# Recurrence inputs fetched ahead, and narrow levels packed, in a decoder trunk on one core

## The chip, the core and the metric

The kernel runs on one core of a Trainium2 chip. A core has a matrix engine (TensorE, PE in the views; its weight loads are listed apart as PEld), VectorE (DVE), ScalarE (ACT), GpSimd (POOL) and SyncE (SP), which here issues DMAs. The metric is the device time of one launch in microseconds, as the median of several runs. Lower is better.

## What is computed

One layer of a hybrid decoder for a prompt of 2048 tokens and eight samples of eight tokens. A normed input is projected by one wide matrix; half of the heads do sparse attention, the other half a gated linear recurrence; then come the output projection and an MLP. What matters here is the recurrence of the prompt, four heads with a 128x128 state each:

```python
f = lb + (1.0 - lb) * jax.nn.sigmoid(f_logit)
logf = jnp.log(f)
k = 1.0 - f
def step(S, inp):
    qc, kc, vc, gc = inp
    b = jnp.cumsum(gc, axis=2)
    inter = jnp.einsum('bhtd,bhdv->bhtv', qc * jnp.exp(b), S)
    diff = b[:, :, :, None, :] - b[:, :, None, :, :]
    decay = jnp.exp(jnp.where(mask[:, :, None], diff, -jnp.inf))
    A = jnp.einsum('bhtd,bhtsd,bhsd->bhts', qc, decay, kc)
    o = inter + jnp.einsum('bhts,bhsv->bhtv', A, vc)
    bl = b[:, :, -1:, :]
    S = jnp.exp(bl[:, :, 0])[..., None] * S + jnp.einsum('bhsd,bhsv->bhdv', kc * jnp.exp(bl - b), vc)
    return S, o
```

The kernel uses chunks of 128 tokens, 16 of them.

## The kernel before

The stages follow one another: `projections`, then `attention`, whose first part is `recurrence_prompt`, and later `output_and_mlp`. Between stages, and at the end of `recurrence_prompt`, all engines meet.

**Projections.** Four tiles `i` of 512 tokens, each with 28 steps `p`. A step multiplies two of the eight row blocks of one of seven column groups (`kv`, `rg`, `rf`, `q`, `rq`, `qi`, `ri`, four steps each) by all 512 tokens, 24 matmuls. Every step needs its 128x1024 piece of weights in two parts: the high part (`hi`, L332) by ScalarE, the low part (`lo`, L480) by VectorE from the high one, both two steps ahead. `hi(g)` waits until TensorE is done with step g-2. Steps 12 to 19 also carry the forget gate of one head after another: in even steps VectorE turns exp(-z) into f (`forget`, L511, L512, L544); in odd steps ScalarE makes k and log f (L443, L445) ahead of its `hi`, and VectorE runs the scan that gives b (`decay`, L549) behind its `lo`. k goes to the scratch `rkT` and b to `rbT`, by SP. In steps 19 to 26 of tiles 0 to 2 TensorE turns the next tile's rows (L671), and VectorE makes their low part (`turned_low`, L501, tile `hT`). In tile 2 VectorE also does so for the sample's rows in step 19 (L653), and in tile 3 each step has eight or four further matmuls for the sample.

**The prompt's recurrence.** A chunk's pair weights A are built by levels. A level l splits the tokens into groups of 2m = 2 << l; its factors are exp(ref - (b - log k)) for the earlier half of a group and q * exp(b - ref) for the later half, with ref the b between the halves. One matmul per head gives all products of a level, and VectorE picks those that belong to it into `pair_weights` (`copy_predicated`, L1115 and L1121). The order of levels is 6, 5, 0, 1, 2, 3, 4. The two widest are put by small matmuls over the k·q product into one bank (L1170, L1177), and picked together (the joined pick); the other five are matmuls of 128x128 by 128 (L1185), with a bank and a pick each. There are four banks for six slots.

Per chunk GpSimd subtracts (12 instructions, L961 and L962), ScalarE takes exponentials (L1008, L1009, L1015), and VectorE multiplies the later halves by q (L1132). ScalarE also takes log k (L991) and VectorE subtracts it from b (L1100), for the next chunk; GpSimd waits for that. Then come q·exp b (L1127), the decayed keys and their transposes (L997, L1193, L1031), the outputs (L1203, L1204), the new state (L1208, L1061), the norm (L975 to L1079) and the gate (`mix`, L1087). Each engine's order is the order of the code, chunk by chunk; chunks 0, 1, 14 and 15 are written out and the others are a loop of two.

SP loads k, b, q, v and the gate's rows two chunks ahead, one queue, in the order of `next_inputs`; between the loads for chunks 2 and 3, and again between those for 3 and 4, stand the sample's small loads (`index_inputs`, L897 to L906). The first loads of the stage are issued at its start. Ahead of the chunks GpSimd has two memsets and four indirect gathers, and VectorE makes the gathers' indices (L1046 to L1052).

## Time and profile before

| | us |
|---|---|
| median of 3 runs | 4038.43 |
| lowest and highest | 4038.22, 4041.91 |
| the profiled execution's own time | 4044.13 |
| its span | 4042.4 |
| projections, in the span | 0 to 680.8 |
| prompt's recurrence, in the span | 680.8 to 914 |

| engine | busy us | share of the span |
|---|---|---|
| TensorE | 3576.2 | 88% |
| VectorE | 2794.6 | 69% |
| ScalarE | 2219.3 | 55% |
| GpSimd | 1048.2 | 26% |

The busy shares are averages over stages. In a timeline row the first number is the start in us from the span's start, the second the length from the first to the last of a merged group; brackets hold the idle time ahead of the group and what ended it. In a row of waits the numbers are the sum of the waits in us, how many, and the longest. In a row by stretch each engine has busy time and the number of instructions; PEclk is the granted clock of TensorE, where 1.00 is its upper level of 2.4 GHz and 0.50 the lower of 1.2 GHz.

### The profile page before, as it was taken

The numbers are of one execution on the slowest core, as the hardware profiler recorded it, in microseconds if no ns is written. First come the engines' busy times: TensorE is split into PE (matmuls) and PEld (weight loads), VectorE is DVE, ScalarE is ACT, GpSimd is POOL, SyncE is SP. The second block draws the span as 40 slices with busy tenths as digits, with TensorE's granted clock in tenths as the row PEclk, the third lists the DMA queues.
The fourth block names the chain that finished last, engine by engine and source line by source line (L and its number), as shares of the span: only waits on it lengthen the run. The fifth ranks groups of instructions, "written<-read, shape, count | busy, mean of one in ns | idle before, by whom it ended". The sixth has DMA issues, their size and how long they took to land. (4 is left out here: it accounts for less than half of the span.)

```text
span 4042.4 us, 52687 instructions
## 1 busy us (share of the span) xinstructions
PE 3576.2 (88%) x18026; PEld 2856.8 (71%) x18027; DVE 2794.6 (69%) x4745; ACT 2219.3 (55%) x3701; POOL 1048.2 (26%) x1120
## 2 busy tenths in 40 slices
PE   8999998889777489875599998989999998999998
PEld 7878786777655235454488886868888887888886
DVE  6675655887888789888678885665556544555565
ACT  3333323776678589887567774335455444443232
POOL 0000001664311011100256730215556551000011
PEclk9999998999877799986699999989999999999999
DMA  6555444435200244424456633567667656554464
GB/s 170 166 150 156 132 125 149 118 102 157 64 23 21 73 148 173 157 99 122 121 197 216 222 132 131 198 215 222 191 218 233 201 179 197 183 186 147 137 217 138
DMA packets 387885, 624.83 MB, mean 155 GB/s; under 512 B 97560, under 2 KB 216440, under 8 KB 379320
## 3 DMA queue, kind: packets, MB, share of 16 engines
q1 hardware_dynamic: 309848, 312.05, 26.0%
q0 software_dynamic: 77376, 309.63, 22.9%
q8 instruction: 137, 2.24, 0.2%
q14 instruction: 108, 0.88, 0.1%
q10 hardware_dynamic: 416, 0.02, 0.0%
HBM read 444.81 MB, written 176.77 MB: 154 GB/s over the span
## 5 line engine op out<-in xcount | busy, mean ns | idle before, releaser
L3814 PE MATMUL up_acc<-x_parts_first,w_up_parts 128*128 128x512 f32 x1536 | 361.4, 395 | 14.1 <-DVE w_up_parts L3564 14.1
L738 PE MATMUL accumulated<-hT,w_in_parts 128*128 128x512 f32 x1536 | 361.3, 395 | 2.1 <-DVE w_in_parts L480 2.1
L3814 PEld LDWEIGHTS up_acc<-x_parts_first,w_up_parts 128*128 128x128 f32 x1536 | 293.3, 191 | 76.6 <-DVE w_up_parts L3564 15.3
L738 PEld LDWEIGHTS accumulated<-hT,w_in_parts 128*128 128x128 f32 x1536 | 290.6, 190 | 65.3 <-DVE w_in_parts L480 3.8
L2800 DVE TENSOR_SCALAR_CACHE_REDUCE junk_dve<-score,candidate 128x2048 bf16<-128x2048 f32 (+6 forms) x224 | 328.5, 1505 | 8.5 <-DVE candidate L2786 8.0
L3905 PE MATMUL down_acc<-w_down_parts_even,hidden_parts 128*128 128x512 f32 x1344 | 314.6, 391 | 14.0 <-DVE hidden_parts L3600 11.8
L3905 PE MATMUL down_acc<-w_down_parts_odd,hidden_parts 128*128 128x512 f32 x1344 | 312.7, 390 | 0.0
L3905 PEld LDWEIGHTS down_acc<-w_down_parts_even,hidden_parts 128*128 128x128 f32 x1344 | 252.9, 189 | 68.3 <-issue 15.9
L2723 ACT ACTIVATE junk_act<-score,candidate 128x1920 bf16<-128x1920 f32 (+6 forms) x224 | 286.4, 1294 | 19.6 <-DVEq L2787 15.6
L3366 ACT ACTIVATE hidden_parts<-hidden_raw 128x1024 fp32r<-128x1024 f32 x112 | 118.6, 1059 | 312.3 <-PE down_acc L3905 289.8
L3905 PEld LDWEIGHTS down_acc<-w_down_parts_odd,hidden_parts 128*128 128x128 f32 x1344 | 251.8, 188 | 53.2 <-issue 1.0
L332 ACT ACTIVATE w_in_parts<-w_in_raw 128x1024 fp32r<-128x1024 f32 (+1 forms) x112 | 113.6, 1014 | 296.5 <-PE accumulated L734 121.2
L480 DVE TENSOR_TENSOR w_in_parts<-w_in_raw,w_in_parts 128x1024 fp32r<-128x1024 f32 (+1 forms) x112 | 130.8, 1169 | 203.4 <-ACT w_in_parts L332 202.1
L3564 DVE TENSOR_TENSOR w_up_parts<-up_raw,w_up_parts 128x512 fp32r<-128x512 f32 x224 | 176.0, 786 | 113.0 <-ACT w_up_parts L3344 111.5
L734 PE MATMUL accumulated<-w_in_parts,hT 128*128 128x512 f32 (+1 forms) x1152 | 239.5, 366 | 1.7 <-DVE hT L501 1.7
L2108 DVE TENSOR_TENSOR probs_T<-p_T,probs_T 128x512 fp32r<-128x512 f32 x272 | 183.8, 688 | 73.7 <-ACT probs_T L2032 72.3
L734 PEld LDWEIGHTS accumulated<-w_in_parts,hT 128*128 128x128 f32 x1152 | 200.2, 188 | 32.3 <-issue 3.2
L3600 DVE TENSOR_TENSOR hidden_parts<-hidden_raw,hidden_parts 128x1024 fp32r<-128x1024 f32 x112 | 138.1, 1233 | 111.9 <-ACT hidden_parts L3366 111.6
L2032 ACT ACTIVATE probs_T<-p_T 128x512 fp32r<-128x512 f32 x272 | 156.9, 594 | 94.1 <-PE p_T L1968 93.1
L1390 PE MATMUL dots<-ki_high,qi_parts 128*128 128x512 f32 (+3 forms) x304 | 146.8, 485 | 68.9 <-ACT relu L1412 67.1
L3263 POOL DMA_DIRECT2D hidden_raw<-scratch_hs x112 | 60.1, 537 | 536.4 <-DVE hidden_parts L3600 536.4
L1459 DVE SCALAR_TENSOR_TENSOR score<-relu,wi,score 128x1024 f32<-128x1024 f32 (+7 forms) x154 | 180.4, 1171 | 24.5 <-ACT relu L1412 7.7
(541 smaller groups left out, 8685.2 us busy)
## 6 DMA issues: line engine op xcount, KB each, us to landing
hidden_raw<-scratch_hs POOLq DMA_DIRECT2D x112, 512.0 KB, 4.6
w_in_raw<-in_w_in SPq DMA_DIRECT2D x80, 512.0 KB, 4.1
up_raw<-scratch_ws SPq DMA_DIRECT2D x128, 256.0 KB, 2.9
scratch_hs<-hidden_even POOLq DMA_DIRECT2D x112, 256.0 KB, 5.0
scratch_hs<-hidden_odd POOLq DMA_DIRECT2D x112, 256.0 KB, 4.9
up_raw<-in_w_up SPq DMA_DIRECT2D x96, 256.0 KB, 5.6
weight_sums<-in_w_down POOLq DMA_DIRECT2D x16, 1024.0 KB, 5.3
scratch_wt<-weight_sums POOLq DMA_DIRECT2D x16, 1024.0 KB, 5.7
```

The source lines that it names most:

```text
L734: mm = pe.matmul(z, h[:, a, k, n * P:(n + 1) * P], w2[:, g % 2, b, k2 * w:(k2 + 1) * w], start=(first and j == 0), stop=(last and j == 2))
L738: mm = pe.matmul(z, w2[:, g % 2, b, k2 * ST + n * P:k2 * ST + (n + 1) * P], h[:, a, k, :], start=(first and j == 0), stop=(last and j == 2))
L1390: pe.matmul(dots[:, u % DB, c:c + w], qs[:, b, h, :], kh[:, k], start=True, stop=False)
L1459: dve.scalar_tensor_tensor(s, r, wi[:, i, h:h + 1], s, ALU.mult, ALU.add).then_inc(acc_done, 1)
L2032: act.activation(ET[:, s % 3, 0, :], pT[:, turn_at[s] % 3, :], ACT.Copy).then_inc(th_rdy, 1)
L2108: dve.tensor_tensor(ET[:, s % 3, 1, :], pT[:, turn_at[s] % 3, :], ET[:, s % 3, 0, :].bitcast(F32), ALU.subtract).then_inc(tl_rdy, 1)
L2723: act.activation(ja[:, n % 2, 0:WIDTH[i]], score[:, SOFF[i]:SOFF[i + 1]], ACT.Sign, bias=cf[:, c:c + 1], accum_out=cnt[:, c:c + 1]).then_i ...
L2800: dve.tensor_scalar(jd[:, n % 2, 0:WIDTH[i]], score[:, SOFF[i]:SOFF[i + 1]], cf[:, c:c + 1], None, ALU.is_ge, ALU.add, accum_out=cnt[:, c: ...
L3564: dve.tensor_tensor(out, raw[:, g % RAW, :], high.bitcast(F32), ALU.subtract).then_inc(lo_rdy, 1)
L3600: dve.tensor_tensor(ap[:, s % A_PARTS, 1, :], araw[:, s % A_RAW, :], ap[:, s % A_PARTS, 0, :].bitcast(F32), ALU.subtract).then_inc(a_lo, 1)
L3814: mm = pe.matmul(up_bank(n), wp[:, n % SLOTS, b, q * P:(q + 1) * P], X(i)[:, a, q, :], start=(q == 0 and (a, b) == (0, 0)), stop=(q == QUA ...
L3905: mm = pe.matmul(down_bank(s), ap[:, s % A_PARTS, a, j * P:(j + 1) * P], B(ph)[:, j, b, :], start=(j == 0 and (a, b) == (0, 0)), stop=(j = ...
```

## The change

1. **b less log k.** Projections now compute it: ScalarE takes `Ln` of `k_stage` into the tile `exp_neg_g`, VectorE subtracts it from the scan's b in place, and SP stores it to a new scratch `rbkT`. The recurrence loads it with b; its own `log_k` and `less_log_k` are gone, and GpSimd waits for the load only.
2. **Three wide levels in one bank.** The order is 6, 5, 4, 0, 1, 2, 3. Levels 4, 5 and 6 share the bank and the pick of the k·q product; TensorE waits for the third multiply, and then does level 4 first, in 16 matmuls of 16 by 16. Slots go from six to five.
3. **Packed later halves.** For levels 0 to 3 the multiply by q writes the later halves into the new tile `later_factors`. The level's matmul streams these 64 columns a head, and the pick reads 256 packed columns.
4. **Fetched inputs.** The recurrence's inputs for chunks 0 and 1, its masks and the identity are loaded by GpSimd's queue in tile 3 of the projections, in 15 DMAs, into memory that tile 2's `hT` has left. SP's own first loads are gone. GpSimd's memsets move behind chunk 0 and its gathers behind chunk 1; the index arithmetic on VectorE moves behind chunk 0.

The diff, cut to its core:

```diff
 # projections: SP, GpSimd, ScalarE, VectorE
+                    if p in (14, 16, 18, 20):
+                        c = (p - 14) // 2
+                        sp.wait_ge(bk_rdy, 4 * i + c + 1)
+                        out(sc["rbkT"][c, :, tok], exg[:, c, :], bk_out[c])
...
+                pool.wait_ge(w_used, PER * END)
...
+                for par in range(2):
+                    own = slice(par * P, (par + 1) * P)
+                    for dst, src in (("r_k", "rkT"), ("r_b", "rbT"), ("b_less_log_k", "rbkT"), ("r_q", "rqT")):
+                        pool.dma_start(head[dst][:, par, :, :], sc[src][:, :, own].rearrange("h p t -> p h t")).then_inc(head_in, 16)
...
                             act.activation(fw[:, 1, :], fw[:, 0, :], ACT.Ln).then_inc(ln_done, 1)
+                            act.wait_ge(k_rdy, 4 * i + c + 1)
+                            act.wait_ge(g_rdy, 4 * i + c + 1)
+                            act.activation(exg[:, c, :], kst[:, c % 2, :], ACT.Ln, bias=least[:, 0:1]).then_inc(lnk_done, 1)
                         hi(PER * i + p + 2)
...
                     dve.tensor_tensor_scan(bst[:, c % 2, :], smask[:, :], fw[:, 1, :], 0.0, ALU.mult, ALU.add).then_inc(b_rdy, 1)
+                    dve.wait_ge(lnk_done, 4 * i + c + 1)
+                    dve.wait_ge(b_rdy, 4 * i + c + 1)
+                    dve.tensor_tensor(exg[:, c, :], bst[:, c % 2, :], exg[:, c, :], ALU.subtract).then_inc(bk_rdy, 1)
 # recurrence
-    ORDER = [6, 5, 0, 1, 2, 3, 4]
-    SLOTS = LEVELS - 1
+    ORDER = [6, 5, 4, 0, 1, 2, 3]
+    JOINED = 3
+    SLOTS = 1 + LEVELS - JOINED
...
+                    turned(bk, "rbkT", g, par, b_in)
                     turned(bt, "rbT", g, par, b_in)
...
-                    pool.wait_ge(b_in[par], 16 * j + 16)
-                    pool.wait_ge(bk_rdy, g + 1)
+                    pool.wait_ge(b_in[par], 32 * j + 32)
...
-                            if not is_last(g):
-                                log_k(g + 1, j + par, 1 - par)
...
-                        dve.tensor_tensor(x, x, qs, ALU.mult).then_inc(x_rdy, 1)
-                        if n >= 2:
-                            pick(n - 2)
+                        if n < JOINED:
+                            dve.tensor_tensor(x, x, qs, ALU.mult).then_inc(x_rdy, 1)
+                        else:
...
+                            dve.tensor_tensor(later[:, n - JOINED, :, :].rearrange("p h t -> p (h t)").rearrange("p (n m) -> p n m", m=1 << ORDER[n]),
+                                              x, qs, ALU.mult).then_inc(x_rdy, 1)
+                        if n >= JOINED:
+                            pick(n - JOINED)
...
                             middle(g + 1, j + par, 1 - par)
-                            less_log_k(g + 1, 1 - par)
...
-                    for n in range(2):
+                    pe.wait_ge(x_rdy, LEVELS * g + JOINED)
+                    for n in reversed(range(JOINED)):
                         m = 1 << ORDER[n]
-                        pe.wait_ge(x_rdy, LEVELS * g + n + 1)
...
-                            x = X[:, ORDER[slot + 1], h * P:(h + 1) * P]
-                            mm = pe.matmul(o[:, h * P:(h + 1) * P], x, x, start=True, stop=True)
+                            x = X[:, ORDER[slot + JOINED - 1], h * P:(h + 1) * P]
+                            mm = pe.matmul(o[:, h * P // 2:(h + 1) * P // 2], x, later[:, slot - 1, h, :], start=True, stop=True)
```

On VectorE, in an odd step of tile 1 of the projections, before:

```order
L544 TENSOR_SCALAR forget<-exp_neg,lb_work 128x512
L480 TENSOR_TENSOR w_in_parts<-w_in_raw,w_in_parts 128x1024
L549 SCALAR_TENSOR_TENSOR b_stage<-scan_mask,forget 128x512
L485 TENSOR_SCALAR row_stats<-row_stats 128x4
L480 TENSOR_TENSOR w_in_parts<-w_in_raw,w_in_parts 128x1024
```

and after:

```order
L571 TENSOR_SCALAR forget<-exp_neg,lb_work 128x512
L507 TENSOR_TENSOR w_in_parts<-w_in_raw,w_in_parts 128x1024
L576 SCALAR_TENSOR_TENSOR b_stage<-scan_mask,forget 128x512
L579 TENSOR_TENSOR exp_neg_g<-b_stage,exp_neg_g 128x512
L512 TENSOR_SCALAR row_stats<-row_stats 128x4
L507 TENSOR_TENSOR w_in_parts<-w_in_raw,w_in_parts 128x1024
```

The subtract (`exp_neg_g<-b_stage,exp_neg_g`) stands between the scan and the low part of the following step's weights.

On TensorE, the levels of chunk 1 of the recurrence, before:

```order
L1170 MATMUL levels<-r_q,r_k 128x128 x4
L1177 MATMUL levels<-level_factors 64x64 x4
L1177 MATMUL levels<-level_factors 32x32 x8
L1185 MATMUL levels<-level_factors 128x128 x12
L1193 MATMUL kd_T<-identR,k_decayed 128x128 x4
L1185 MATMUL levels<-level_factors 128x128 x8
```

and after:

```order
L1187 MATMUL levels<-r_q,r_k 128x128 x4
L1194 MATMUL levels<-level_factors 16x16 x16
L1194 MATMUL levels<-level_factors 32x32 x8
L1194 MATMUL levels<-level_factors 64x64 x4
L1202 MATMUL levels<-later_factors,level_factors 128x64 x12
L1208 MATMUL kd_T<-identR,k_decayed 128x128 x4
L1202 MATMUL levels<-later_factors,level_factors 128x64 x4
```

Sixteen products of 16 by 16 come in ahead, four of 128 columns go, and the rest of these stream 64 columns; behind the transposes stands one level where two stood. The program's matmuls count once here, and twice in the trace, where each is two instructions.

## Rows read from the trace of the kernel before

**Rows 1.** Waits from 20 to 680 us: sum, times, longest (us)

```profile
PE accumulated L671 <- DVE hT L501: 10.1, 6, 1.9
PE accumulated L671 <- DVE hT_sample L653: 3.9, 1, 3.9
```

**Rows 2.** Timeline of VectorE in tile 1 of the projections

```profile
252.60 1.23 DVE L480 TENSOR_TENSOR w_in_parts<-w_in_raw,w_in_parts 128x1024 fp32r<-128x1024 f32 x1 [2.26 <-ACT w_in_parts L332]
...
266.27 1.23 DVE L480 TENSOR_TENSOR w_in_parts<-w_in_raw,w_in_parts 128x1024 fp32r<-128x1024 f32 x1 [1.02 <-ACT w_in_parts L332]
...
295.64 0.74 DVE L501 SCALAR_TENSOR_TENSOR hT<-accumulated,gain_pre_mix,hT 128x512 fp32r<-128x512 f32 x1
```

**Rows 3.** Timeline of TensorE in tiles 1 and 2

```profile
288.83 5.73 PE L738 MATMUL accumulated<-hT,w_in_parts 128*128 128x512 f32 x24 [1.07 <-DVE w_in_parts L480]
296.44 0.66 PE L671 MATMUL accumulated<-identA,x_sb 128*128 128x128 f32 x4 [1.87 <-DVE hT L501]
296.86 7.34 PE L738 MATMUL accumulated<-hT,w_in_parts 128*128 128x512 f32 x24
...
450.22 7.73 PE L738 MATMUL accumulated<-hT,w_in_parts 128*128 128x512 f32 x24
```

**Rows 4.** Busy time by stretch: us, then each engine, clock, DMA share, GB/s

```profile
296.80:304.20 7.40, 7.40 (x29) 5.89 (x28) 5.76 (x5) 0.69 (x1) 0.00 (x0) 0.77 0.40 106
...
786.00:812.00 26.00, 21.36 (x204) 19.44 (x202) 22.54 (x55) 20.57 (x65) 18.61 (x24) 1.00 0.40 121
```

**Rows 5.** Timeline of one chunk in the loop

```profile
804.63 2.63 DVE L1132 TENSOR_TENSOR level_factors<-level_factors,r_q 128x256 f32<-128x256 f32 x3
...
805.88 1.06 PE L1177 MATMUL levels<-level_factors 128*64 128x64 f32 x24
...
807.19 0.72 DVE L1115 COPY_PREDICATED pair_weights<-level_mask_joined,levels 128x512 f32<-128x512 int32 x1
...
807.81 0.41 DVE L1132 TENSOR_TENSOR level_factors<-level_factors,r_q 128x256 f32<-128x256 f32 x1
...
814.81 0.42 DVE L1121 COPY_PREDICATED pair_weights<-level_masks_second,levels 128x256 f32<-128x256 int32 x1
...
815.28 0.49 PE L1203 MATMUL o<-state,q_exp_b 128*128 128x128 f32 x2 [0.99 <-DVE pair_weights L1121]
```

**Rows 6.** Groups by form, 786 to 812.35 us: busy us, mean ns, idle before

```profile
L991 ACT ACTIVATE log_k<-r_k,least_k 128x512 f32<-128x512 f32 x2 | 1.4, 710 | 0.0
L1100 DVE TENSOR_TENSOR b_less_log_k<-r_b,log_k 128x512 f32<-128x512 f32 x2 | 1.4, 684 | 0.0
```

**Rows 7.** Timeline of chunk 0 of the recurrence

```profile
686.49 0.69 DVE L1100 TENSOR_TENSOR b_less_log_k<-r_b,log_k 128x512 f32<-128x512 f32 x1
...
687.22 0.35 ACT L1008 ACTIVATE level_factors<-b_less_log_k,r_b 128x64 f32<-128x64 f32 x1 [1.65 <-DVE b_less_log_k L1100]
...
691.49 0.64 POOL L961 TENSOR_TENSOR less_ref<-r_b,b_less_log_k 128x256 f32<-128x256 f32 x1
...
699.74 0.63 ACT L1015 ACTIVATE level_factors<-less_ref 128x512 f32<-128x512 f32 x1 [0.57 <-POOL less_ref L962]
...
706.84 0.46 PE L1203 MATMUL o<-state,q_exp_b 128*128 128x128 f32 x2 [0.77 <-DVE pair_weights L1121]
```

**Rows 8.** Timeline of TensorE: first outputs of chunks 1, 2, 3 and 15

```profile
719.65 0.46 PE L1203 MATMUL o<-state,q_exp_b 128*128 128x128 f32 x2 [1.04 <-DVE pair_weights L1121]
...
736.53 0.49 PE L1203 MATMUL o<-state,q_exp_b 128*128 128x128 f32 x2 [0.75 <-DVE pair_weights L1121]
...
750.20 0.49 PE L1203 MATMUL o<-state,q_exp_b 128*128 128x128 f32 x2 [1.00 <-DVE pair_weights L1121]
...
904.77 0.46 PE L1203 MATMUL o<-state,q_exp_b 128*128 128x128 f32 x2 [0.75 <-DVE pair_weights L1121]
```

**Rows 9.** Timeline of ScalarE in chunk 2

```profile
726.52 0.72 ACT L991 ACTIVATE log_k<-r_k,least_k 128x512 f32<-128x512 f32 x1 [4.68 <-DMA r_k<-scratch_rkT]
```

**Rows 10.** Timeline of TensorE: groups of small matmuls

```profile
660.79 1.00 PE L704 MATMUL accumulated<-foldA,x_sb 128*128 128x64 f32 x8
...
693.89 0.64 PE L1177 MATMUL levels<-level_factors 128*32 128x32 f32 x16 [3.02 <-DVE level_factors L1132]
```

More of the change, by code:

```diff
@@ L84, in own_semaphores, with projections @@
         stage(nc, *args)
-def projections(nc, io, sc):
+def projections(nc, io, sc, head):
     RAW = 3
@@ L795, in recurrence_prompt @@
         sb, ps, sem = memory(nc, ctx)
-        qt, kt, bt = (sb(n, [P, 2, RH, P]) for n in ("r_q", "r_k", "r_b"))
-        vt, gt = sb("r_v", [P, 2, RH, P]), sb("r_g", [P, 2, RH, P])
-        ident = sb("identR", [P, P])
-        joined = sb("level_mask_joined", [P, 1, P], I32)
-        second = sb("level_masks_second", [P, SLOTS - 1, RH * P // 2], I32)
-        lk, least = sb("log_k", [P, RH, P]), sb("least_k", [P, 1])
-        bk = sb("b_less_log_k", [P, 2, RH, P])
+        qt, kt, bt, bk, vt, gt = (head[n] for n in ("r_q", "r_k", "r_b", "b_less_log_k", "r_v", "r_g"))
+        ident, joined, second = (head[n] for n in ("identR", "level_mask_joined", "level_masks_second"))
+        sb("head_inputs", [P, (HEAD_SKIP + HEAD_BYTES - BEFORE_HEAD) // 4])
         mid = sb("minus_b_mid", [P, 2, RH])
@@ L830, in recurrence_prompt, with chunks @@
         qb, wd, kn = (ahead[n] for n in ("qi_blocks", "wi_rows", "ki_new"))
-        def chunks(eng, body):
+        def chunks(eng, body, between=None):
             for par in range(2):
                 body(par, 0, par)
+                if between:
+                    between(par)
             with eng.Fori(1, NCH // 2 - 1) as j:
@@ L1148, in _, with index_rows @@
                 middle(0, 0, 0)
-                less_log_k(0, 0)
-                chunks(dve, body)
+                def index_rows(par):
+                    if par == 1:
+                        return
+                    pages, odd, base = (ahead[n] for n in ("pages", "odd_half", "base"))
+                    dve.wait_ge(x_pages, 32)
+                    dve.tensor_scalar(base[:, 0, :], pages[:, :], 16.0, odd[:, 0:1], ALU.mult, ALU.add).then_inc(x_base, 1)
+                    dve.tensor_scalar(base[:, 1, :], pages[:, :], 8.0, odd[:, 1:2], ALU.mult, ALU.add).then_inc(x_base, 1)
+                    dve.wait_ge(x_base, 2)
+                    for c in range(8):
+                        dve.tensor_scalar(gidx[:, :, c], base[:, 0, :], float(c), None, ALU.add).then_inc(x_idx, 1)
+                    for c in range(4):
+                        dve.tensor_scalar(gkv[:, :, c], base[:, 1, :], float(c), None, ALU.add).then_inc(x_idx, 1)
+                chunks(dve, body, index_rows)
                 add_state(NCH - 1, 1)
@@ L1241, with attention @@
 PROBS_SKIP = 136000
-def attention(nc, io, sc):
+HEAD_SKIP, BEFORE_HEAD = 49152, 8800
+HEAD_TILES = (*((n, [P, 2, RH, P], F32) for n in ("r_q", "r_k", "r_b", "b_less_log_k", "r_v", "r_g")), ("identR", [P, P], F32),
+              ("level_mask_joined", [P, 1, P], I32), ("level_masks_second", [P, LEVELS - 3, RH * P // 2], I32))
+HEAD_BYTES = 4 * sum(math.prod(shape[1:]) for _, shape, _ in HEAD_TILES)
+def attention(nc, io, sc, head):
     with ExitStack() as ctx:
@@ L1269, in attention @@
                      "ident": at("identP", [P, P])[:, :], "fold": at("foldP", [P, DH])[:, :]}
-        own_semaphores(nc, recurrence_prompt, io, sc, gidx, gkv, ahead)
+        own_semaphores(nc, recurrence_prompt, io, sc, gidx, gkv, ahead, head)
         with ExitStack() as pctx:
@@ L3975, in constants @@
             "bucket_of": (np.arange(BUCKETS)[:, None] == bucket[None, :]).astype(np.float32),
[L3976 removed]
+            "levels": lev.astype(np.int32), "levels_joined": (lev[:, 0:1] | lev[:, 5:6] | lev[:, 6:7] | lev[:, 7:8]).astype(np.int32), "levels_second": second, "later": (s > t).astype(np.int32)}
 def views(io):
@@ L3991, in trunk @@
     io = views(io)
-    own_semaphores(nc, projections, io, sc)
-    attention(nc, io, sc)
+    with ExitStack() as place:
+        at = memory(nc, place)[0]
+        at("head_skip", [P, HEAD_SKIP // 4])
+        head = {n: at(n, shape, dt) for n, shape, dt in HEAD_TILES}
+    own_semaphores(nc, projections, io, sc, head)
+    attention(nc, io, sc, head)
     own_semaphores(nc, output_and_mlp, io, sc)
```

120 lines of the change are left out of this document (54 added, 66 removed).

## The prediction

> **What bounds the kernel now.** I read the page's busy slices first (TensorE is near full except in two places), then the stretches, then the waits of the two stages that the diff touches, then their timelines. The change edits only the projections (0 to 680.8 us of the span) and the prompt's recurrence (680.8 to 914), which run one after the other with a barrier between and after them. So a microsecond lost or won in either moves the end of the span by about as much, and the sum is made per stage.
>
> The projections look bound by TensorE, but where TensorE stands still, VectorE is late: it waits for `hT` and for the sample's `hT` [rows 1]. In tile 1 VectorE is on a chain without a gap: weights' low parts (`lo`), `forget`, a round trip through ScalarE (k, Ln, then the high part of the next weights) that VectorE waits 2.26 us for, `lo`, scan [rows 2]. It has one piece of slack in the phase, 1.02 us at 266.27, and its last link, the subtract of hT that ends at 296.38, releases TensorE [rows 2, 3]. The stall also costs clock: the 24 products behind it take 7.34 us, where 5.7 is usual (the group at 288.83 takes that), because the granted clock falls to 0.77 over that stretch; after the 3.94 us stall of tile 2 it is 7.73 us [rows 3, 4].
>
> In the recurrence no engine is full: of 26.0 us (two chunks) VectorE is busy 22.5, TensorE 21.4, ScalarE 20.6, GpSimd 18.6 [rows 4]. One chunk takes 12.9 us, by a ring: the last pick of a chunk releases TensorE's outputs, new state, k·q and wide levels (about 4.7 us), while VectorE does mix, q·exp b and three multiplies; then picks and multiplies alternate with TensorE's levels up to the next last pick [rows 5].
>
> **Added to the projections.** Each of 4 tiles by 4 heads gets one more Ln of 128x512 on ScalarE, between the Ln of forget and the weights' high part, and one more subtract of 128x512 on VectorE behind the scan. Same shapes now take 710 and 684 ns [rows 6]; successive instructions overlap by some 0.09, so 0.62 and 0.61 on the engine. The subtract needs the scan to have ended, and loses that overlap and a semaphore's time: 0.13. Both lie on the chain above, since VectorE waits for ScalarE's high part: 1.36 us a head, 5.4 a tile. Tiles 0 and 1 have the 1.0 us of slack once: +4.4 each. Tile 2 has sample work in that place, and TensorE waits at its end for the sample's hT, which VectorE reaches late [rows 1]; only 0.25 is absorbed: +5.2. A longer stall should leave more of the following step at the low clock, as 7.73 against 7.34 shows: +0.4 in tiles 0 and 1. In tile 3 TensorE's steps are longer for the sample's products, and the chain has gaps of 2 to 3.5 us: +0.2. Sum **+15.0**. Below: 12, if ScalarE's Ln hides in the wait for k and the clock costs nothing. Above: 17, if tile 3 or the clock takes more. The 16 stores of `rbkT` stand on SP's queue behind loads that already wait for a later `lo`, so nothing waits for them. The 15 fetches on GpSimd's queue run in tile 3, where that engine is idle, and move 3 MB beside weights loaded two steps ahead: 0.
>
> **Taken from the recurrence's start.** Today the first loads are issued at 680.8; b less log k starts at 686.49, the wide factors at 687.22, and GpSimd, behind four indirect gathers, starts at 691.49; the last exponential of chunk 0 starts at 699.74 and its outputs at 706.84 [rows 7]. With inputs there at 680.8, ScalarE has its table and exp b by 682.7, the wide factors by 684.7; GpSimd starts at once, its first two pairs are ready in time, and the rest follow the exponentials by 1.4 us a pair, to a last exponential at about 691.3. Then multiplies, three narrow levels, transposes and the last level: outputs at about 695.5 at full clock. TensorE is cold here, so I take 696.3: **-10.5** (-8 to -12). VectorE's 14 small index instructions move behind chunk 0; TensorE's outputs, state and k·q of chunk 0 cover most of their 1.5 us. The gathers move behind chunk 1 and make GpSimd 1.3 us late for chunk 2, and in chunk 1 the loop's shorter form gains it back: **-0.3** for chunk 1.
>
> **Chunks 2 and 3.** Outputs start at 706.84, 719.65, 736.53, 750.20: chunk 2 takes 16.9 us, chunk 3 takes 13.7 [rows 7, 8]. ScalarE waits 4.68 us for r_k, whose load stands behind 20 sample loads on SP [rows 9]. log k and this wait go. Next late is b and b less log k of chunks 3 and 4, queued behind the same sample loads; with the whole stage 11 us earlier they land about when `minus_b_mid` wants them. With GpSimd's 1.3 us and about 1 us for chunk 3's b: **-3.7** (-1 to -4.7).
>
> **The loop, 12 more chunks.** Take the end of the third multiply as 0. Today the joined pick starts within 0.47 us of it and the last pick ends at +8.0 [rows 5]. Changed: VectorE loses the subtract (0.61) and one pick (0.34), ScalarE the Ln (0.62). But TensorE now starts the wide levels only after the third multiply, and has 32 more narrow matmul instructions. The present 24 (8 of 64 columns, 16 of 32) take 1.06 [rows 5], of which the last instruction's own length is 0.2; split by columns that is 0.053 and 0.027 apart, and even at the low clock 16 of 32 columns take 0.64, at most 0.03 apart [rows 10]. So 16 columns cost 0.013 each if the spacing falls further, 0.027 if not: 0.4 to 0.9, I take 0.65. So the joined pick starts at +1.95, and state, multiplies and picks follow; pick 2 waits for TensorE (1.4 after its multiply), the last pick starts at +7.85 and ends at +8.3. Halving the moving columns gains nearly nothing: 8 instructions that load 128 columns and stream 64 take 1.00 us [rows 10], the same as eight of 128. What shortens the ring is the other part: GpSimd no longer waits for VectorE's b less log k and works while VectorE picks, so q·exp b and the first multiply run uncontended; the three multiplies take 2.6 us beside GpSimd now [rows 5], but 0.41 us each alone. Third multiply at +12.1 to +12.5, and TensorE's k·q ends at +12.0, so there is no more than that to win. 12.3 against 12.88 (904.77 less 750.20, by 12) is **-7.0**; between 12.0 and 12.9, so -10.6 to 0.
>
> On the narrow products, the trace has no 16-column form, and its spacing falls with the columns down to 32 [rows 5, 10]. The Trainium skill, TensorE: Matmul & The Clock Gate, Back-to-back issue gap, states a floor of about 25 ns for 1 to 64 columns; by it the 32 would cost 0.8 us and the loop's gain would be 5 us; no run here shows it yet.
>
> **Sum.** 15.0 - 10.5 - 0.3 - 3.7 - 7.0 = -6.5 us. The profiled execution took 4044.1 (span 4042.4), so 4037.6 by its own time; the median of the runs is 4038.4, so **4031.9**.
>
> **Rivals.**
> - *The loop stays at 12.9.* Contention moves from the first multiplies to the later ones, since GpSimd's two early pairs fall beside them, and the ring is as long as before. For: the last pick ends at +8.3 against +8.0, later than today. Against: GpSimd idles 7.4 us in 26 [rows 4]. Gives 15.0 - 14.5 = +0.5: 4039. Chance 0.22.
> The Trainium skill, Advanced Engine Details and Errata, VectorE Performance Modes, says that VectorE's second SBUF port is shared with GpSimd and the two block each other; the 2.6 us for three multiplies agree, and by the rule work that moves beside other multiplies gives the loss back there, which is this rival.
> - *More gained, or less lost.* The loop reaches 12.0 (TensorE's bound), or VectorE's added work costs 12 and not 15. For: I place most waits at their worst. Gives -13, up to -18 with both: 4025, down to 4020. Chance 0.28.
> - *Narrow products dominate.* The 32 instructions of 16 columns sit in the ring, before the joined pick, with nothing beside them. If each costs as much as one of 128 columns, 0.107, they take 3.4 us for my 0.65, times 14 chunks, +38: 4070. It turns the sum slower by 8 us from 0.053 each. Against: the 32-column ones go at 0.027. A milder way to the same side is a late b for several chunks. Chance 0.10.
> - *Forecast*: chance 0.40.
>
> **Numbers.** 4031.9. A measurement of this kernel tells about 0.2% (8.1 us) from no change, so the threshold is 4030.3, close to my sum: a third of the forecast's own chance lies beyond it. Faster 0.28 + 0.13 = 0.41; same 0.27 + 0.22 = 0.49; slower 0.10. Range: 4022 (both gains larger, all but the far end) to 4044 (loop unchanged, projections 17, start -8).
>
> **What would show it.** The projections' end at about 696 for 680.8; TensorE's stall before the turned rows longer by 2 us or more in tiles 0 to 2, with `w_in_parts` at odd steps waiting 2.9 us for 2.26. The first outputs 15 to 16 us after the barrier, for 26. No wait for r_k in chunks 2 and 3. In the loop, 12.3 us from output to output; the joined pick waiting over 1 us; narrow products (56 instructions) in 1.5 to 2.0 us. Wrong would be: no shift of the projections' end (ScalarE and VectorE had cover that I missed), or a loop over 13 us.

## The result, and the profile after

The changed kernel took 4077.9 us (median of four runs, 4072.7 to 4085.5) against 4039.6 us for the kernel before, run beside it: a ratio of 1.0094, with a 95% interval of 1.0081 to 1.0106. The forecast was 4031.9 us; its range ended at 4044, and slower had a chance of 0.10. The profiled execution of the changed kernel took 4073.4 us, 4.5 less than its median, and that of the kernel before 4044.1, 4.5 more than its median. The spans, 4071.5 us against 4042.4, so differ by 29 us and not by the medians' 38, and the traces explain these 29.

| us from the span's start | before | changed | e1 | e3 | e7 |
|---|---|---|---|---|---|
| VectorE's first instruction of the recurrence | 680.85 | 692.88 | 692.34 | 692.36 | 677.21 |
| first outputs, chunk 0 | 706.84 | 710.05 | 707.55 | 707.19 | 693.09 |
| first outputs, chunk 3 | 750.20 | 754.12 | 749.46 | 750.47 | 735.55 |
| first outputs, chunk 15 | 904.77 | 931.94 | 904.48 | 904.75 | 890.18 |
| TensorE's first instruction of the next stage | 917.49 | 947.15 | 917.16 | 917.43 | 902.89 |
| span | 4042.4 | 4071.5 | 4041.7 | 4042.9 | 4028.8 |

e1, e3 and e7 are experiments that follow. First the loop of twelve chunks by stretch, in the kernel before:

```profile
750.20:904.77 154.57, 127.40 (x1200) 116.05 (x1201) 133.37 (x323) 119.99 (x375) 108.83 (x140) 1.00 0.38 112
```

and in the changed kernel:

```profile
754.12:931.94 177.82, 149.51 (x1488) 141.89 (x1489) 127.29 (x300) 114.91 (x367) 109.68 (x140) 0.77 0.37 112
```

What follows the recurrence is the same to 0.6 us (3124.9 and 3124.4 us, by the table). The loop grew by 23.3 us, 14.82 us a chunk for 12.88, and the third number from the end of its row points at why: TensorE's granted clock was 1.00, and is 0.77. One chunk of the changed kernel, TensorE's timeline; L1202 are the packed products:

```profile
785.61 0.63 PE L1218 MATMUL o<-state,q_exp_b 128*128 128x128 f32 x2
...
788.84 1.30 PE L1194 MATMUL levels<-level_factors 128*16 128x16 f32 x56
790.07 1.10 PE L1202 MATMUL levels<-later_factors,level_factors 128*128 128x64 f32 x8
792.44 2.14 PE L1202 MATMUL levels<-later_factors,level_factors 128*128 128x64 f32 x16 [1.27 <-DVE later_factors L1137]
...
795.23 1.81 PE L1202 MATMUL levels<-later_factors,level_factors 128*128 128x64 f32 x8
```

and the clock over it, by stretch:

```profile
788.00:792.00 4.00, 3.17 (x73) 2.81 (x71) 2.74 (x8) 2.25 (x5) 4.00 (x6) 1.00 0.51 149
792.00:798.00 6.00, 4.89 (x29) 4.70 (x30) 3.78 (x14) 3.15 (x12) 1.87 (x3) 0.69 0.40 119
798.00:801.50 3.50, 3.50 (x19) 3.50 (x19) 3.17 (x7) 2.90 (x10) 2.42 (x3) 0.55 0.40 128
801.50:805.50 4.00, 3.93 (x79) 3.56 (x78) 2.65 (x5) 3.05 (x11) 4.00 (x6) 1.00 0.47 149
```

The clock is at the upper level (2.4 GHz) when outputs, state and k·q have just run; it falls to the lower one (1.2 GHz) during the packed products, and comes back only in the next chunk's outputs and state. So the same eight packed products take 1.10 us and 1.81 us within one chunk, and two outputs 0.63 us for the 0.39 of a chunk that starts at the upper level (at 769.01). At full clock the 56 narrow products take 1.30 us for the 1.06 us of 24 [rows 5]: the rival that I feared is not there, 32 more cost 0.24 us.

The projections end 12.0 us later. TensorE's waits in them (sum, times, longest), in the kernel before one that [rows 1] leaves out:

```profile
PE accumulated L738 <- DVE w_in_parts L480: 2.1, 2, 1.1
```

and in the changed kernel the three largest:

```profile
PE accumulated L769 <- DVE w_in_parts L507: 9.8, 14, 2.2
PE accumulated L702 <- DVE hT L528: 8.9, 10, 1.7
PE accumulated L702 <- DVE hT_sample L684: 6.1, 1, 6.1
```

VectorE's timeline in tile 1 of the changed kernel:

```profile
256.61 1.23 DVE L507 TENSOR_TENSOR w_in_parts<-w_in_raw,w_in_parts 128x1024 fp32r<-128x1024 f32 x1 [2.87 <-ACT w_in_parts L357]
...
259.07 0.69 DVE L579 TENSOR_TENSOR exp_neg_g<-b_stage,exp_neg_g 128x512 f32<-128x512 f32 x1
...
268.15 1.23 DVE L507 TENSOR_TENSOR w_in_parts<-w_in_raw,w_in_parts 128x1024 fp32r<-128x1024 f32 x1 [2.87 <-ACT w_in_parts L357]
```

As the prediction had it, the round trip through ScalarE takes 2.87 us for 2.26 [rows 2], and the new subtract stands behind the scan; a head takes 11.54 us. The lateness shows at w_in_parts (9.8 us for 2.1); at hT, where the prediction looked for it in tiles 0 and 1, TensorE waits no longer than before (8.9 us for 10.1).

### The profile page after: what moved, and what is told of

The parts are those of the page before. It is cut to its first block and busy times, and to the rows that moved or that the text cites. A ratio compares the mean times of both kernels' runs of the same rounds, so it can differ in the third digit from the quotient of the medians.

```text
span 4071.5 us, 53472 instructions
## 1 busy us (share of the span) xinstructions
PE 3604.1 (89%) x18410; PEld 2886.5 (71%) x18411; DVE 2794.0 (69%) x4729; ACT 2220.3 (55%) x3701; POOL 1058.9 (26%) x1135
## 3 DMA queue, kind: packets, MB, share of 16 engines
q8 instruction: 138, 2.26, 0.2%
```

## The experiments

Medians are of 4 to 11 runs each, ratios to the kernel before run in the same comparison (medians 4041.7, 4040.9 and 4041.4 us for e1 to e4, e5 to e8, e9 to e12), with 95% intervals. The theory after the first look: the halved products cost nothing in time and take the clock away.

**e1, full width.** In the changed kernel:

```diff
-mm = pe.matmul(o[:, h * P // 2:(h + 1) * P // 2], x, later[:, slot - 1, h, :], start=True, stop=True)
+twice = later[:, slot - 1, h:h + 1, :].to_broadcast([P, 2, P // 2])
+mm = pe.matmul(o[:, h * P // 2:h * P // 2 + P].rearrange("p (n m) -> p n m", n=2), x, twice, start=True, stop=True, skip_group_check=True)
```

> The changed kernel with one edit: each product of a single level (L1202) streams 128 columns again, its 64 packed ones twice, so that TensorE streams as many columns there as in the kernel before; its output, VectorE's work and every wait are as in the changed kernel. Theory A (TensorE's granted clock falls in the loop because the halved products give it less to stream): the clock of the loop goes from 0.79 back to about 0.97, the chunk from 14.8 to about 13.4 us, the total from 4078 to about 4060. Rival B (it falls because TensorE stands idle before the later joined pick, whatever it streams): clock and total stay, 4073 to 4083. Rival C (the low clock is the chip's own state and not the kernel's doing): clock varies from run to run without regard to the edit.

Measured: 4045.6 us, ratio 1.0013 [1.0004, 1.0022], so 32 us less than the changed kernel, and lower than theory A had given. By stretch:

```profile
749.46:904.48 155.02, 118.39 (x1488) 108.23 (x1489) 126.64 (x300) 115.12 (x370) 108.86 (x140) 1.00 0.43 129
```

TensorE's waits from 749.4 to 904.5 us:

```profile
PE levels L1203 <- DVE later_factors L1137: 18.1, 21, 1.5
PE levels L1194 <- DVE level_factors L1133: 10.4, 12, 1.5
PE o L1219 <- DVE pair_weights L1121: 8.8, 13, 0.8
```

One group of its products:

```profile
797.56 1.16 PE L1203 MATMUL levels<-later_factors,level_factors 128*128 128x128 f32 x8 [0.26 <-DVE later_factors L1137]
```

The clock is 1.00 and the chunk 12.92 us. TensorE waits longer here, 37.3 us over the loop, than in the changed kernel (18.1, 2.1 and 8.8 for the same three waits), and is busy for 76% of the time against 84%. These sums alone would not settle rival B, since the low clock itself lengthens what TensorE does and so shortens its waits. So take one chunk in each from the first outputs on, both at the upper level. The changed kernel, then what followed at once:

```profile
768.46:777.00 8.54, 6.78 (x102) 6.34 (x102) 7.19 (x19) 6.98 (x25) 6.45 (x9) 1.00 0.51 154
...
777.40:782.89 5.49, 4.61 (x22) 4.24 (x22) 2.84 (x8) 2.93 (x12) 2.23 (x4) 0.50 0.33 96
```

and e1, the same piece and then the whole chunk:

```profile
762.57:771.10 8.53, 6.81 (x101) 6.32 (x102) 7.18 (x19) 6.89 (x24) 6.51 (x9) 1.00 0.52 154
...
762.57:775.12 12.55, 9.91 (x124) 9.03 (x124) 10.47 (x26) 9.58 (x32) 9.16 (x12) 1.00 0.49 146
```

TensorE stands still for 1.76 us in the one piece and 1.72 in the other, and only in the changed kernel does the clock fall after it. Rival B falls. What the halving saved is 0.06 us in eight products (1.10 for 1.16).

**e2, the kernel before with half width.**

```diff
-mm = pe.matmul(o[:, h * P:(h + 1) * P], x, x, start=True, stop=True)
+_, xs, _ = halves(x, ORDER[slot + 1])
+_, os, _ = halves(o[:, h * P:(h + 1) * P], ORDER[slot + 1])
+mm = pe.matmul(os, x, xs, start=True, stop=True, skip_group_check=True)
```

> The kernel before with one edit: each product of a single level (L1185) streams only the 64 columns that the pick reads, read and written with a stride in their old places; nothing is packed, nothing else moves. Theory A: the loop's clock falls below 0.9 and its chunk grows from 12.9 to over 13.5 us: total 4038 + 8 to + 20. Rival B: TensorE waits no longer than before, so the clock stays at 0.99 and the total at 4036 to 4040.

Measured: 4089.4 us, ratio 1.0121 [1.0106, 1.0137]. More than expected: this edit alone, which takes work away, costs 48 us. Its loop by stretch:

```profile
755.95:943.28 187.33, 164.26 (x1200) 154.85 (x1201) 131.88 (x323) 118.85 (x372) 103.86 (x140) 0.76 0.31 93
```

and eight of its products at either level, in TensorE's timeline:

```profile
782.54 1.11 PE L1187 MATMUL levels<-level_factors 128*128 128x64 f32 x8 [0.83 <-DVE level_factors L1132]
...
829.40 1.81 PE L1187 MATMUL levels<-level_factors 128*128 128x64 f32 x8
```

**e5, other products in the gaps.** In the changed kernel, before slot 2 and before the outputs:

```diff
+for h in range(RH):
+    pe.matmul(o[:, h * P:(h + 1) * P], ident[:, :], vt[:, par, h, :], start=True, stop=True, skip_group_check=True)
```

> The changed kernel with packed products of 64 columns as they are, plus 8 products in each chunk that nobody reads (identity times r_v, 128 columns, 16 matmul instructions), put where TensorE waits: four before its wait for the second single level, four before its wait for the last pick. They add as many columns as the packing took away. Theory A (the clock follows how much TensorE streams, in whatever form): the loop's granted clock returns to 0.97 or more, the chunk to 13.0 to 13.6 us (the fillers may delay the outputs by up to 0.5), total 4046 to 4056. Rival D (it is the 64-column form itself, its instructions too short for their 128-column weight loads): clock stays near 0.8, and the fillers run at the low clock too and lengthen the chunk: 4078 or more.

Measured: 4052.1 us, ratio 1.0026 [1.0015, 1.0038]; 26 us less than the changed kernel for 16 instructions more a chunk, on whose results nothing rests. The loop by stretch:

```profile
754.52:907.40 152.88, 135.41 (x1682) 128.07 (x1681) 123.68 (x301) 114.99 (x369) 109.15 (x140) 1.00 0.44 132
```

Clock 1.00, and 12.74 us a chunk. Rival D falls: the 64-column form itself does no harm. By itself e5 would also fit rival B, since the fillers take up waits; it is e1 that excludes B. With three kernels changed in opposite directions and the clock following each time, rival C falls too: the mean clock of the whole span is 0.919 to 0.927 in all eight runs of the changed kernel and e2, and 0.933 or more in every run of every other kernel. Chunk 0 pays for the fillers: 19.6 us from the barrier to the outputs at a clock of 0.50, for 15.2 at 0.63 in e1. So from the barrier to the next stage e5 takes 227.3 us for e1's 224.8, although its loop is shorter; the medians are 6.5 us apart, and the rest of that is open.

**e3, two wide levels and nothing packed.** The multiply in place, the waits of the narrow products and the strided pick are also as in the kernel before; b less log k from the projections and the fetch remain.

```diff
-ORDER = [6, 5, 4, 0, 1, 2, 3]
-JOINED = 3
+ORDER = [6, 5, 0, 1, 2, 3, 4]
+JOINED = 2
...
-mm = pe.matmul(o[:, h * P // 2:(h + 1) * P // 2], x, later[:, slot - 1, h, :], start=True, stop=True)
+mm = pe.matmul(o[:, h * P:(h + 1) * P], x, x, start=True, stop=True)
```

> The changed kernel without the three joined levels and without the packed halves: b less log k from the projections and the fetched inputs remain, the levels are multiplied, put through TensorE and picked as in the kernel before. Projections 12 us longer, first outputs 8 to 9 us sooner after the barrier than in the kernel before, chunks 2 and 3 some 4 us shorter, the loop 12.9 us a chunk or a little less, without subtract and Ln (12.5): sum -0.5 to -6. Total 4033 to 4040. Were the loop's loss due to b less log k coming from memory rather than to the narrow products, the total would stay above 4060.

Measured: 4045.2 us, ratio 1.0012 [1.0003, 1.0021], 5 to 12 us above what was expected. Outputs come 14.8 us after the barrier for 26.0 (-11.2). But chunks 2 and 3 take 30.76 us for 30.55, and the loop 12.86 us a chunk: the subtract and the Ln are gone from it, and it is no shorter. Its time equals e1's, so the third wide level and the packing, with full columns, are together worth nothing that shows. GpSimd's timeline ahead of chunk 2:

```profile
715.34 1.02 POOL L987 DMA_INDIRECT ki_rows<-in_cache_idx_k,gather_idx  x1 [0.16 <-issue]
...
719.19 0.94 POOL L987 DMA_INDIRECT ki_rows<-in_cache_idx_k,gather_idx  x1 [0.30 <-issue]
```

and VectorE's in chunk 2:

```profile
722.67 5.36 DVE L1131 TENSOR_TENSOR level_factors<-level_factors,r_q 128x256 f32<-128x256 f32 x3
```

**e8, the gathers behind the last chunk.** e3 with this in GpSimd's program:

```diff
-                    else:
-                        pool.wait_ge(x_idx, 12)
-                        for n in range(4):
-                            pool.indirect_dma_start(ahead["ki_rows"][:, n, :], None, io["cache_idx_k"][0].rearrange("a (c r) d -> (a c) (r d)", c=16),
...
                 chunks(pool, body, index_rows)
+                pool.wait_ge(x_idx, 12)
+                for n in range(4):
+                    pool.indirect_dma_start(ahead["ki_rows"][:, n, :], None, io["cache_idx_k"][0].rearrange("a (c r) d -> (a c) (r d)", c=16),
...
```

> e3_two_wide_unpacked with the four gathers of index rows put behind the last chunk. In e3 chunk 2 took 18.2 us while GpSimd, 4.8 us late behind the gathers, subtracted beside VectorE's multiplies (5.36 us for three). If the gathers cause that: chunk 2 in 13 to 14 us, total 4 to 5 us below e3, 4041. If chunk 2 is long for a late r_b or r_k: no change.

Measured: 4042.2 us, ratio 1.0003 [0.9994, 1.0012], 3 us below e3. The same three multiplies take 2.57 us:

```profile
724.86 2.57 DVE L1130 TENSOR_TENSOR level_factors<-level_factors,r_q 128x256 f32<-128x256 f32 x3
```

and outputs 1 to 3 are 27.44 us apart (722.62 to 750.06) for 30.76. So the four gathers, 4.8 us on GpSimd, had eaten what chunks 2 and 3 would have won.

**e6 and e9, less on GpSimd.** Both are e3 with less work for GpSimd from chunk 1 on (chunk 0 keeps both lines); the factors are then made from old differences. e6 leaves out the second subtraction of each level, e9 replaces both by one of four columns:

```diff
+if isinstance(g, int) and g == 0:
...
+else:
+    pool.tensor_tensor(of, ref, kf, ALU.subtract).then_inc(sub_done, 2)
```

```diff
+if isinstance(g, int) and g == 0:
...
+else:
+    pool.tensor_tensor(dif[:, n % 2, 0:4], bt[:, par, 0, 0:4], bt[:, par, 0, 0:4], ALU.subtract).then_inc(sub_done, 2)
```

> e3_two_wide_unpacked with GpSimd's second subtraction of each level (L978 there, 128x256) left out from chunk 1 on, so that the upper halves of the factors are made from older differences and the result is not the reference's; all waits remain. Theory (the loop stays at 12.86 us in e3 because GpSimd works beside VectorE and stretches its multiplies: q times exp b 1.04 to 1.10 us for 0.69, three multiplies 2.6 for 1.2): the multiplies shorten and the chunk falls to 12.0 to 12.4 us, total 5 to 10 us below e3. Rival (the loop is bound by the alternation of VectorE and TensorE and not by GpSimd): 12.8 us, total as e3, 4045.

> e3_two_wide_unpacked with GpSimd's two subtractions of each level replaced by one of four columns from chunk 1 on: its load is gone from the loop, all waits remain, the factors are made from old differences and the result is not the reference's. With half of that load gone (e6) the chunk fell from 12.86 to 12.61 us only, though the three multiplies were still 2.6 us. If contention with GpSimd is what keeps the loop long, the multiplies of all levels fall to 0.41 us and the chunk to 12.0 or less (total 4033 or less). If TensorE's outputs, state, k.q and joined levels (5.1 us from the last pick to the joined one) cover the early multiplies and only the later ones count, the chunk is 12.2 to 12.6 us and the total 4036 to 4041.

Measured: e6 4041.0 us, ratio 1.0000 [0.9991, 1.0009], 12.61 us a chunk; e9 4036.1 us, ratio 0.9987 [0.9978, 0.9996]. e9's outputs of chunks 4 to 13 are 12.14 us apart (874.59 less 765.29, by 9). Both chunks lie between what the two theories had given; e9's total is at the low end of the second theory's. VectorE's groups by form from 763.6 to 891.5 us, some ten chunks, in the kernel before:

```profile
L1132 DVE TENSOR_TENSOR level_factors<-level_factors,r_q 128x256 f32<-128x256 f32 x70 | 44.0, 651 | 0.0
...
L1127 DVE TENSOR_TENSOR q_exp_b<-r_q,exp_b 128x512 f32<-128x512 f32 x10 | 7.8, 777 | 4.9 <-DVE mix_rows L1087 4.9
```

in e3:

```profile
L1131 DVE TENSOR_TENSOR level_factors<-level_factors,r_q 128x256 f32<-128x256 f32 x70 | 48.4, 713 | 0.0
...
L1126 DVE TENSOR_TENSOR q_exp_b<-r_q,exp_b 128x512 f32<-128x512 f32 x10 | 10.5, 1046 | 5.3 <-DVE mix_rows L1093 5.3
```

and in e9:

```profile
L1134 DVE TENSOR_TENSOR level_factors<-level_factors,r_q 128x256 f32<-128x256 f32 x73 | 28.6, 416 | 0.0
...
L1129 DVE TENSOR_TENSOR q_exp_b<-r_q,exp_b 128x512 f32<-128x512 f32 x11 | 7.6, 692 | 5.5 <-DVE mix_rows L1096 5.5
...
L1117 DVE COPY_PREDICATED pair_weights<-level_mask_joined,levels 128x512 f32<-128x512 int32 x10 | 7.4, 739 | 18.0 <-PE levels L1190 18.0
```

Taking the subtract (6.9 us in ten chunks) off VectorE left its other multiplies longer by 7.1 us (4.4 and 2.7), which ate all of it. That they contend with GpSimd is shown by e9: with GpSimd's load gone a multiply takes 416 ns for 713. The Trainium skill, Advanced Engine Details and Errata, VectorE Performance Modes, says that GpSimd and VectorE's two-port instructions block each other at a shared port; the 416 ns for 713 agree with blocking, but which port these multiplies use no run here shows. The chunk only falls to 12.14 us, because VectorE then waits 1.8 us a chunk for TensorE's joined levels (the last row). So both causes hold, in turn: GpSimd for 0.7 us, and TensorE behind it.

**e4 and e7, the fetch alone.** e4 is e3 with the change's part of the projections taken back, and in the recurrence's loop, on ScalarE and on VectorE:

```diff
+log_k(g + 1, j + par, 1 - par)
...
+less_log_k(g + 1, 1 - par)
```

e7 is e4 with the gathers as in e8, and in `less_log_k`

```diff
 dve.wait_ge(lk_rdy, g + 1)
-dve.wait_ge(mid_rdy, g + 1)
+dve.sem_inc(spare, 1)
```

> The kernel before with only the inputs of the first two chunks and the constants fetched during the projections (and the index rows moved behind chunks 0 and 1); log k and the subtract stay in the recurrence. Projections as before (0), first outputs 6 to 9 us sooner after the barrier, chunk 2 perhaps still waiting for r_k: total 4028 to 4034, so 4 to 10 us faster than before. If the fetch on GpSimd's queue disturbs the projections' weights, it is 4038 or more.

> e4_fetched_only with the four gathers of index rows put on GpSimd's queue behind the last chunk, where it is idle, and without the extra wait for minus_b_mid that e4's subtract had. If the gathers (4.8 us on GpSimd in chunk 2) and that wait explain why e4 gained 3 us and not 10: chunk 2 in 13.5 us for 16.1 in before's and e4's pattern, loop 12.9 us for e4's 13.4, total 4026 to 4032. If the loop's 13.4 us in e4 has another cause, it stays at 13.4 and the total at 4034 to 4038.

Measured: e4 4038.6 us, ratio 0.9993 [0.9984, 1.0002], 5 us above the expected range; e7 4032.2 us, ratio 0.9981 [0.9972, 0.9991], just above its own. Outputs 15.9 us after the barrier in both. e4's loop takes 13.39 us a chunk and e7's 12.89; which of e7's two edits gave this was not separated, though e3 and e8, which differ by the gathers alone, have nearly the same loop (12.86 and 12.83). e7 beats both kernels.

**e10 and e11, the projections' part alone.** e10 is e7 with Ln, subtract and store of the change in the projections, read by nobody:

```diff
+act.wait_ge(k_rdy, 4 * i + c + 1)
+act.wait_ge(g_rdy, 4 * i + c + 1)
+act.activation(exg[:, c, :], kst[:, c % 2, :], ACT.Ln, bias=least[:, 0:1]).then_inc(lnk_done, 1)
...
+dve.wait_ge(lnk_done, 4 * i + c + 1)
+dve.wait_ge(b_rdy, 4 * i + c + 1)
+dve.tensor_tensor(exg[:, c, :], bst[:, c % 2, :], exg[:, c, :], ALU.subtract).then_inc(bk_rdy, 1)
```

and e11 is e10 without the last three of these lines; the store waits for `lnk_done` there.

> e7_fetched_late_rows plus the projections' part of the change alone: Ln of k, subtract and store of b less log k, which the recurrence does not read. It prices that part with the recurrence unchanged. By the prediction's chain (both on the way of VectorE's next weights): +15 us, between 12 and 17: total 4044 to 4049. By the profiled runs so far (barrier at 691.5 to 695.0 with it, 677.2 to 680.9 without): 12 to 15. If part of the loss was the transfer of the result or its fetch, less than 10.

> e10_both_places without VectorE's subtract: ScalarE's extra Ln and the store remain in the projections, the recurrence is as in e7. If the chain runs through ScalarE's high part to VectorE's low part, as the prediction has it, Ln costs 0.6 us of the 1.36 a head: about 6 us over e7, total 4037 to 4040. If Ln hides behind VectorE's own work and the subtract alone is late: 0 to 2 us over e7. If ScalarE is the bound: as e10.

Measured: e10 4049.0 us, ratio 1.0021 [1.0012, 1.0030]; e11 4038.3 us, ratio 0.9993 [0.9984, 1.0002]. So 16.8 and 6.1 us above e7. The recurrence's first VectorE instruction in e7's timeline:

```profile
677.21 0.06 DVE L1055 MEMSET least_k<- 128x1 f32 x1 [13.04 <-PEq L83]
```

in e11's:

```profile
685.06 0.06 DVE L1064 MEMSET least_r<- 128x1 f32 x1 [13.06 <-PEq L83]
```

and in e10's:

```profile
692.93 0.06 DVE L1067 MEMSET least_r<- 128x1 f32 x1 [13.09 <-PEq L83]
```

By these single traces 7.9 us for each of the two instructions, by the medians 6.1 for the Ln and 10.7 for the subtract. Equal projections end up to 3.6 us apart between traces (the section below), so the split is rough; but neither share is nothing, and both instructions lie on the chain.

**e12, e7 with fillers.** The kernel that ran differs from e7 by e5's fillers alone, behind a condition:

```diff
+def filler(o):
+    if not (isinstance(g, int) and g == 0):
+        for h in range(RH):
+            pe.matmul(o[:, h * P:(h + 1) * P], ident[:, :], vt[:, par, h, :], start=True, stop=True, skip_group_check=True)
...
+if slot == 2:
+    filler(o)
...
+filler(bank_free(SLOTS))
```

> e7_fetched_late_rows with the three joined levels and the packed halves of the change, and in every chunk but the first the 8 products that nobody reads, as in e5: the projections without the change's part, log k and subtract in the loop. e5's loop took 12.74 us a chunk against 12.92 in e1, and e7's 12.89: if the same 0.15 to 0.2 us is won here, the total is 2 us below e7, 4030. If the subtract is late for the longer wait at the joined pick, the chunk is 13.0 or more and the total 4034 or more.

The expectation speaks of the three joined levels and the packed halves as well. They are not in this kernel: its order is 6, 5, 0, 1, 2, 3, 4 with two wide levels, and its single levels stream 128 columns. So it tests another thing than was expected of it. Two of its groups in TensorE's timeline, a single level and a filler:

```profile
781.87 1.16 PE L1208 MATMUL levels<-level_factors 128*128 128x128 f32 x8
782.86 1.06 PE L1187 MATMUL levels<-r_v,identR 128*128 128x128 f32 x8
```

Measured: 4029.9 us, ratio 0.9973 [0.9963, 0.9983], the lowest median of all. Its interval overlaps with e7's, and its loop is 12.90 us a chunk for e7's 12.89, so the 2 us between their medians are not from there. The loops of e7 and of e12 by stretch:

```profile
735.55:890.18 154.63, 127.38 (x1200) 116.04 (x1201) 132.71 (x323) 119.87 (x375) 112.90 (x144) 1.00 0.39 116
...
737.90:892.64 154.74, 146.63 (x1393) 136.67 (x1393) 132.76 (x323) 119.89 (x375) 113.13 (x144) 1.00 0.40 116
```

Where the clock is 1.00 already, the fillers win nothing and cost nothing: TensorE is busy for 95% of the loop and not 82%, and the loop takes the same. The packed halves with fillers and without the projections' part were not measured.

## Why the prediction was wrong, step by step

| term | predicted | changed kernel's trace | full columns, e1's trace | other kernels |
|---|---|---|---|---|
| projections | +15.0 | +12.0 | +11.5 | +15.7 (e10 over e7) |
| start, barrier to outputs | -10.5 | -8.8 | -10.8 | -11.2 (e3) |
| chunk 1 | -0.3 | +2.2 | -0.6 | -0.3 (e3) |
| chunks 2 and 3 | -3.7 | -1.5 | -0.9 | +0.2 (e3), -3.1 (e8) |
| loop | -7.0 | +23.3 | +0.5 | -0.3 (e3) |
| last chunk to next stage | 0 | +2.5 | 0.0 | |
| the rest | 0 | -0.6 | -0.4 | |
| sum | -6.5 | +29.1 | -0.7 | |

**The step that failed** is the one on the halved columns: "Halving the moving columns gains nearly nothing". As a duration it was right (0.06 us). But it priced the products by their length alone. I had the clock in view only where TensorE stands still, and took the loop's 1.00 [rows 4] for granted; no term and no rival had it fall there. e1, e2 and e5 show from three sides that it does: the clock is 0.77 and not 1.00 over the loop, which costs 29 us of the recurrence (254.3 us from barrier to next stage in the changed kernel, 224.8 in e1), and e1's column shows that the start, chunk 1 and the last chunk were late by it too.

**The loop** was mis-sized even at full clock: 12.9 us a chunk (e1) and not 12.3. That is my first rival, contention moves, and I had given it 0.22. VectorE in e1 from 763.6 to 891.5 us, some ten chunks (the kernel before is shown at e9, 44.0 and 7.8 us):

```profile
L1137 DVE TENSOR_TENSOR later_factors<-level_factors,r_q 128x256 f32<-128x256 f32 x40 | 25.7, 642 | 2.9 <-ACT level_factors L1037 2.9
L1133 DVE TENSOR_TENSOR level_factors<-level_factors,r_q 128x256 f32<-128x256 f32 x30 | 24.4, 866 | 0.0
...
L1127 DVE TENSOR_TENSOR q_exp_b<-r_q,exp_b 128x512 f32<-128x512 f32 x10 | 6.9, 693 | 5.3 <-DVE mix_rows L1094 5.3
```

q·exp b does "run uncontended", as the forecast said (693 ns for 777), but the three first multiplies do not get cheap, and the later ones, mostly 0.41 to 0.57 us each before, take 642 ns in the mean. In sum 5.2 of the subtract's 6.9 us come back. I had also seen TensorE's bound and placed it at 12.0; e9 puts it at 12.14 in e3's form.

**Chunks 2 and 3**: I wrote that the gathers make GpSimd "1.3 us late". They are 4.8 us on its queue, at the place where it would work ahead, and cost 3.3 us in e3's form (e3 against e8). The wait for r_k did go; in the changed kernel's trace GpSimd waits 3.5 us for r_b in its place (two waits between 690 and 755 us), in e1's for no load.

**The projections** were right in mechanism and chain (e10, e11), and in size as far as traces can tell. The recurrence's first VectorE instruction comes at 677.2 to 680.9 us in the five traces without this part (before, e2, e4, e7, e12) and at 691.5 to 695.1 in the eight with it (changed, e1, e3, e5, e6, e8, e9, e10): 14.3 us between the means, for a predicted 15.0. The 12.0 of the changed kernel and the 15.7 of e10 over e7 both lie within what equal projections differ by.

The traces show where a part of that comes from: which group of products meets the low clock differs from execution to execution. The stall of 1.87 us ahead of the turned rows was followed by 24 products in 7.34 us in the kernel before [rows 3]; in e7, whose projections do the same work there, it was not:

```profile
294.45 0.66 PE L690 MATMUL accumulated<-identA,x_sb 128*128 128x128 f32 x4 [1.86 <-DVE hT L520]
294.87 5.71 PE L757 MATMUL accumulated<-hT,w_in_parts 128*128 128x512 f32 x24
```

So my +0.4 a tile for a longer stay at the low clock is smaller than this chance. In the changed kernel the new wait, 2.2 us for w_in_parts, stands one group ahead, and the low clock came there:

```profile
295.81 7.35 PE L769 MATMUL accumulated<-hT,w_in_parts 128*128 128x512 f32 x24 [2.23 <-DVE w_in_parts L507]
303.99 0.65 PE L702 MATMUL accumulated<-identA,x_sb 128*128 128x128 f32 x4 [0.83 <-DVE hT L528]
304.40 5.71 PE L769 MATMUL accumulated<-hT,w_in_parts 128*128 128x512 f32 x24
```

and in e8, with the same projections, one group later:

```profile
296.68 5.74 PE L769 MATMUL accumulated<-hT,w_in_parts 128*128 128x512 f32 x24 [2.22 <-DVE w_in_parts L507]
304.86 0.77 PE L702 MATMUL accumulated<-identA,x_sb 128*128 128x128 f32 x4 [2.44 <-DVE hT L528]
305.28 7.29 PE L769 MATMUL accumulated<-hT,w_in_parts 128*128 128x512 f32 x24
```

In front of the turned rows the 1.6 us cost nothing, because TensorE would have waited there for VectorE's hT anyway (0.83 us for 2.44); behind them they are lost. The changed kernel's trace did not lose them in tiles 0 and 1 and the trace before did, twice, which is most of the 3.7 us between 12.0 and 15.7. That is luck, not a saving of the change. By tile (from turned rows to turned rows, tile 3 to the recurrence's first instruction) e10 takes 5.2, 4.6, 5.7 and 0.3 us longer than e7, for a predicted 4.8, 4.8, 5.2 and 0.2. What I had asked for as a sign, a stall before the turned rows longer by 2 us, is found in full in tile 2 only (6.1 for 3.9).

**The start** was right to 0.7 us once the columns are full (-10.8 in e1, -11.2 in e3), and the narrow products were cheaper than my 0.65 us. The Trainium skill, TensorE: Matmul & The Clock Gate, Back-to-back issue gap, would make 32 narrow ones 0.8 us; the rows show 0.24.

Had the loop's clock held, the change would be e1: 4 us slower than before by the medians, since -11 at the start pays for most of the projections and little else is won. Even so its 4045.6 us lie just past the end of my range, 4044.

## What to carry to other kernels

Fewer columns a matmul were not free in a loop whose time is set by other engines: the products took as long as before, and TensorE's clock fell. After narrowing products, read the granted clock of the stretch first of all, and compare with the same products padded back to full width. Work taken off VectorE beside a busy GpSimd can return as longer VectorE instructions; and whatever is moved on a queue must be priced by its whole length there, at the place where that engine runs ahead. A difference of a few us between two single traces can be the place where the low clock fell; compare several traces of equal code before giving it a cause.

## What the runs showed of the hardware

- The granted clock does not follow TensorE's busy share or its waits alone: 1.00 with 76% busy and 37 us of waits in the loop (e1), 0.77 with 84% and 29 us (changed); and after pieces of 8.5 us at the upper level, with 1.76 and 1.72 us of standing still, it fell in the changed kernel and not in e1, which differ in the 64 and 128 columns of the single levels alone. The Trainium skill, TensorE: Matmul & The Clock Gate, The HAM clock gate, puts the fall down to idle time; in the changed kernel's loop no listed wait of TensorE is longer than 1.7 us, and the clock fell.
- 16 instructions a chunk whose results nobody reads made the loop shorter by 2.1 us a chunk where the clock was 0.77 (e5), and left it as it was where the clock was 1.00 (e12 against e7, with TensorE busy for 95% of the time).
- At the upper level eight instructions of 64 columns with 128-column weights take 1.10 us and of 128 columns 1.16 us; at the lower level the former take 1.81 us.
- The same code meets the low clock at different groups in different executions: 24 products behind a stall of 1.87 us took 7.34 us in the kernel before, and behind one of 1.86 us 5.71 us in e7.
- Beside GpSimd's subtractions a 128x256 multiply of VectorE takes 713 ns in the mean (e3), without them 416 (e9).
